# Shift and scale sums of the mixer stages by transposes inside the fourth and the eighth merge block

## The reference

```
mods_x = split(silu(c)     @ ada_w[l] + ada_b[l], 9)     # shift, scale, gate of the three sublayers
mods_c = split(silu(c_ctx) @ ada_w[l] + ada_b[l], 9)
h = layer_norm(s) * (1 + scale) + shift
s = layer_norm(ALPHA * s + w * gate * f(h)) * ln_w + ln_b
```

```
y = (sigmoid(g_ret) * y_ret + sigmoid(g_na) * y_na + sigmoid(g_fou) * y_fou) @ w_o
```

## Time and profile before

| | |
|---|---|
| median of three runs | 2575.18 us |
| the profiled execution | 2576.9 us, span 2575.0 us |
| PE busy | 2453.0 us, 95% of the span |
| DVE busy | 1609.2 us, 62% |
| ACT busy | 936.9 us, 36% |
| shares of the chain that ended last | PE 87%, DVE 8%, ACT 3% |
| mean granted clock of TensorE | 0.975 |

### The profile page before, as it was taken

How to read it: one execution, slowest core, us unless ns; L and a number is a source line. 1 busy time by engine, 2 the same in 40 slices (tenths; PEclk the granted TensorE clock), 3 DMA queues, 4 the chain that set the end, 5 groups by cost and what they waited for, 6 DMA issues and landing times.

```text
span 2575.0 us, 33634 instructions
## 1 busy us (share of the span) xinstructions
PE 2453.0 (95%) x13530; PEld 2120.2 (82%) x13530; DVE 1609.2 (62%) x2146; ACT 936.9 (36%) x1361; POOL 126.0 (5%) x163
## 2 busy tenths in 40 slices
PE   6999999997999999979999999999999899996998
PEld 6988988986876788869889888889888786995996
DVE  4566668756465544576666686666686554665655
ACT  2522355432114322244223554224554223443443
POOL 2000001000001000010000010000020001001000
PEclk9999999999999999989999999999999998997999
DMA  8455555651122343345455565455555242674763
GB/s 263 144 169 166 193 190 175 174 170 33 49 90 58 109 136 123 127 151 164 150 177 194 187 200 173 155 180 188 180 181 173 66 139 70 194 250 131 226 202 123
DMA packets 476814, 400.62 MB, mean 156 GB/s; under 512 B 36340, under 2 KB 428788, under 8 KB 476404
## 3 DMA queue, kind: packets, MB, share of 16 engines
q1 hardware_dynamic: 464992, 391.18, 47.9%
q10 hardware_dynamic: 11668, 7.30, 0.9%
HBM read 397.25 MB, written 1.17 MB: 155 GB/s over the span
## 4 chain that ended last, share of the span: by engine, by line
PE 87%; DVE 8%; ACT 3%; issue 2%; DMA 1%; ACTq 0%; SPq 0%; POOL 0%; POOLq 0%; DVEq 0%
PE ps L1327 25%; PE ps L1328 25%; PE ps L1329 25%; DVE wl L835 2%; PE ps L1585 2%; PE ps L1576 1%; PE ps L1597 1%; PE ps L1525 1%; ACT tB L524 1%; PE ps L1352 1%; ACT wh L506 1%; PE ps L1678 1%; DVE st L893 1%; PE ps L1359 1%; PE ps L1367 1%
## 5 line engine op out<-in xcount | busy, mean ns | idle before, releaser
L835 DVE TENSOR_TENSOR wl<-raw,wh 128x1024 fp32r<-128x1024 f32 x576 | 701.3, 1221 | 678.1 <-ACT wh L506 676.8
L506 ACT ACTIVATE wh<-raw 128x1024 fp32r<-128x1024 f32 x576 | 609.8, 1059 | 1290.1 <-PE ps L1329 1256.9
L1327 PE MATMUL ps<-hh,wh 128*128 128x256 f32 (+1 forms) x2736 | 897.0, 328 | 32.6 <-DVE hl L926 19.8
L1328 PE MATMUL ps<-hl,wh 128*128 128x256 f32 (+1 forms) x2736 | 889.0, 325 | 0.0
L1329 PE MATMUL ps<-hh,wl 128*128 128x256 f32 (+1 forms) x2736 | 888.8, 325 | 0.0
L1327 PEld LDWEIGHTS ps<-hh,wh 128*128 128x128 f32 x2736 | 525.2, 192 | 78.5 <-DVE hl L926 20.9
L1328 PEld LDWEIGHTS ps<-hl,wh 128*128 128x128 f32 x2736 | 525.2, 192 | 41.7 <-issue 1.0
L1329 PEld LDWEIGHTS ps<-hh,wl 128*128 128x128 f32 x2736 | 524.9, 192 | 41.2
L850 DVE SCALAR_TENSOR_TENSOR acc<-araw,c,acc 128x1024 f32<-128x1024 f32 x210 | 258.4, 1280 | 36.3 <-DMA araw<-in_ada_w 34.8
L1327 PE MATMUL ps<-wh,stage_h_f 128*128 128x512 f32 x616 | 240.8, 391 | 2.0 <-DVE stage_l_f L979 2.0
L1328 PE MATMUL ps<-wl,stage_h_f 128*128 128x512 f32 x616 | 239.7, 389 | 0.0
(11 more groups left out here) (160 smaller groups left out, 2388.8 us busy)
## 6 DMA issues: line engine op xcount, KB each, us to landing
raw<-in_ffa_w SPq DMA_DIRECT2D x204, 512.0 KB, 3.6
raw<-in_ffb_w SPq DMA_DIRECT2D x168, 512.0 KB, 3.9
raw<-in_mix_w_in SPq DMA_DIRECT2D x148, 512.0 KB, 4.0
araw<-in_ada_w SPq DMA_DIRECT2D x136, 512.0 KB, 5.1
raw<-in_mix_w_o SPq DMA_DIRECT2D x24, 512.0 KB, 4.3
raw<-in_ret_w_out SPq DMA_DIRECT2D x16, 512.0 KB, 4.0
raw<-in_na_fou_w_out SPq DMA_DIRECT2D x16, 512.0 KB, 3.9
raw<-in_ada_w SPq DMA_DIRECT2D x8, 512.0 KB, 5.2
```

The lines of the kernel that those rows point to most:

```text
L506: A.activation(wh[:, s, :], raw[:, s, :], ACT.Copy).then_inc(w_rounded, 1)
L835: V.tensor_tensor(wl[:, s, :], raw[:, s, :], f(wh[:, s, :]), ALU.subtract).then_inc(w_split, 1)
L1327: T.matmul(out, a[0], b[0], start=start, stop=False)
L1328: T.matmul(out, a[0], b[1], start=False, stop=False)
```

## The change

In both mixers the sums of shift and scale go over to transposes and a DVE sum, one stream at a time, and both are moved into a merge block:

- PE, in blocks `mm` = 3 (shift) and `mm` = 7 (scale): behind unit v, it waits until all of the sum's steps are in `acc` and turns stream 0's eight pieces into banks 6 and 7. Behind unit v+2 it does the same for stream 1, once DVE has taken stream 0 out of the banks (semaphore `mod_taken`). In layer 1 there is stream 0 only.
- DVE, in the same blocks: behind the first gated product it sums stream 0 along the free axis (`mixer_mods`), behind two more splits stream 1, and adds the bias.
- The 16 or 8 one-column matmuls in the fourth block and those behind the eighth go, with their waits. `down` waits for both sums at its start, since its first tile uses banks 6 and 7.

```diff
+            def mixer_mods(i, w, st):
+                t = i + 1
+                ns = htiles(t) // LT
+                c = t % 3 * 3 * KD + w * KD
+                dve.wait_ge(ada_mm, ada_sums(i) + gate_halves(i + 1) - gate_halves(i) + w * ns + st + 1)
+                y = ps[:, 6:8].rearrange("p a n -> p (a n)").rearrange("p (k n) -> p k n", k=KD)
+                V.tensor_reduce(modT[:, t % 2, w, :, st], y, AXX, ALU.add).then_inc(mod_taken, 1)
+                if st == ns - 1:
+                    dve.wait_ge(mod_taken, 4 * (i // 3) + (w + 1) * ns)
+                    ...
+                    V.tensor_tensor(m, m, b, ALU.add).then_inc(mods_ready, 1)
...
                     gated(0, z, 1, 2)
+                    if mm in (3, 7):
+                        mixer_mods(i, mm // 4, 0)
                     split(v + 6)
                     split(v + 7)
+                    if mm in (3, 7) and htiles(i + 1) == NT:
+                        mixer_mods(i, mm // 4, 1)
...
-                    if mm == 3:
-                        next_mods(i, 0, 6)
-                    if mm == 7:
-                        next_mods(i, 1, 2)
-                    else:
+                    if mm < 7:
                         for n in range(2):
                             ada(i, MERGE_ADA + 2 * mm + n)
...
+            def mixer_turn(i, w, st):
+                pe.wait_ge(ada_step, ada_ops[ada0(i) + (w + 2) * KD])
+                before = 4 * (i // 3) + w * (htiles(i + 1) // LT) + st
+                if before:
+                    pe.wait_ge(mod_taken, before)
+                for k in range(KD):
+                    ins = T.transpose(ps[:, 6 + k // 4, (k % 4) * P:(k % 4 + 1) * P], acc[:, st, k * P:(k + 1) * P], ident[:])
+                ins.then_inc(ada_mm, 1)
...
                 if i % 3 == 1:
                     pe.wait_ge(g_sum, 5 + 40 * l + 5 * (KD - 1) + 1)
-                    pe.wait_ge(mods_ready, 2 * (i + 1) + 1)
+                    pe.wait_ge(mods_ready, 2 * (i + 2))
...
                     form_a(v, 0, src, N)
+                    if mm in (3, 7):
+                        mixer_turn(i, mm // 4, 0)
                     pe.wait_ge(g_sum, smn + 1)
...
                     form_a(v + 2, 2, src, N)
-                    if mm == 3:
-                        ada_mods(i, 0, 6)
+                    if mm in (3, 7) and htiles(i + 1) == NT:
+                        mixer_turn(i, mm // 4, 1)
...
-                pe.wait_ge(g_sig, 24 * l + 3 * (KD - 1) + 5)
-                ada_mods(i, 1, 2)
                 down(i, AT["wo", l], KD)
```

More of the change, by code:

```diff
@@ L227, in trunk @@
         ada_step, adab_turned, adab_copied, adab_ready = [sem(n) for n in ("ada_step", "adab_turned", "adab_copied", "adab_ready")]
-        gbias_in, first_mm, ada_mm, gate_ready, mods_ready = [sem(n) for n in ("gbias_in", "first_mm", "ada_mm", "gate_ready", "mods_ready")]
+        gbias_in, first_mm, ada_mm, mod_taken, gate_ready, mods_ready = [sem(n) for n in ("gbias_in", "first_mm", "ada_mm", "mod_taken", "gate_ready", "mods_ready")]
         y_tile, ln_in, post_stat, post_rstd, x_ready = [sem(n) for n in ("y_tile", "ln_in", "post_stat", "post_rstd", "x_ready")]
@@ L345, in chunk_streams, with mod_sums @@
             return streams(s) if w == 2 else htiles(s) // LT
+        def mod_sums(i):
+            return htiles(i + 1) // LT if i % 3 == 1 else 1
         def ada_sums(i):
-            return 1 + gate_halves(i) + 2 * i
+            return 1 + gate_halves(i) + sum(mod_sums(j) for j in range(i)) * 2
         MERGE_ADA = KD + 2
@@ L845, in ada @@
                         if m:
-                            dve.wait_ge(ada_mm, ada_sums(i) + (0, gate_halves(i + 1) - gate_halves(i), gate_halves(i + 1) - gate_halves(i) + 1)[n // KD])
+                            dve.wait_ge(ada_mm, ada_sums(i) + (0, gate_halves(i + 1) - gate_halves(i), gate_halves(i + 1) - gate_halves(i) + mod_sums(i))[n // KD])
                         ins = V.tensor_scalar(acc[:, st], araw[:, m % AR], c, None, ALU.mult)
@@ L884, in turned_mods @@
                 V.tensor_tensor(m, m, b, ALU.add).then_inc(mods_ready, 1)
-            def next_mods(i, w, bank):
-                dve.wait_ge(ada_mm, ada_sums(i + 1) - 1 + w)
-                take_mods(i + 1, w, bank, float(DV))
+            def mixer_mods(i, w, st):
[7 more added lines that the diff above has]
+                    dve.wait_ge(mod_taken, 4 * (i // 3) + (w + 1) * ns)
+                    m = modT[:, t % 2, w, :, 0:ns]
+                    b = adaT[:, t // 3, c:c + KD].unsqueeze(2).broadcast_to([P, KD, ns])
+                    V.tensor_tensor(m, m, b, ALU.add).then_inc(mods_ready, 1)
             def stats(src, which, t, done):
@@ L1412, in down @@
                             pe.wait_ge(g_sum, 5 + 40 * (l + 1))
-                            pe.wait_ge(mods_ready, 2 * (i + 2))
                         else:
```

## The result

The changed kernel takes 2598.23 us (median of 4 runs, 2597.30 to 2598.62) against 2574.85 us (2570.20 to 2578.59) of the kernel before on the same chip: a ratio of 1.0091, with a 95% interval of 1.0074 to 1.0109. It is slower, as forecast (2593.0 us), by 23.4 us in place of 17.8, and 0.23 us above the upper end of the range (2598).

The account below looks back on a forecast made before the run. PE, busy 95% of the span, was taken to bound the kernel. Terms of +1.6, +6.4, +4.0 and +5.8 us at four places summed to +17.8 us, giving a median of 2593.0 us, range 2584 to 2598 us.

Parts of the forecast that it names:

- The wait: Behind unit v in four merge blocks, PE waits for DVE's last sum steps: 3.40 to 3.58 us each, 13.97 us together.
- Transposes against one-column matmuls: In the merge blocks, eight transposes add 0.87 us; removed one-column groups give back 5.20 and 1.78 us in the fourth blocks.
- Start of `down`: Behind the eighth blocks, removed matmuls become a wait for `stage_l_m`; 0.37 us won in layer 0, nothing in layer 1.
- The clock: Behind each of the four new PE waits, a new clock drop costing 1.5 us, bounds nothing and 1.72 us.
- A second term: The two existing clock drops at the start of `down` were let stand, with no change in time.
- Rival 1: At the four places the waits come but the new clock drops don't: +11.8 us, 2587.0 us; chance 0.15.
- Rival 2: Transposes count as quiet time, adding two more 1.5 us low-clock stretches in layer 0: +20.8 us, 2596.0 us; chance 0.09.
- Rival 3: DVE's sums come onto the path, two to four of 1.215 us showing: about 2596.5 us; chance 0.06.
- Rival 4: Sums are in time behind unit v, so no waits: -2.1 us, 2573.1 us, or 2569.7 us; chance 0.05.

Follow-up runs that it names:

- second profile of the changed kernel: The changed kernel run once more with nothing altered, against the kernel before: 2596.99 us, ratio 1.0086.
- the one with the first sum one split earlier: Transposes moved behind units v+2 and v+3, with DVE's stream 0 sum between the splits of v+6 and v+7, against the kernel before: 2576.28 us, ratio 1.0000.
- the first moved version: Changed kernel with transposes moved behind units v+2 and v+3, DVE's stream 0 sum behind the split of v+7: 2590.79 us, ratio 1.0059 to the kernel before.

## Why the prediction was right, and where it was wrong

- **The wait** (forecast 13.97 us): right. It came at the four places, from the releaser named: 13.0 us in PE's idle records, 13.6 us by the starts of the products. With the wait alone added to the old kernel the places lose 20.0 us; with the wait removed by place they win 2.9.
- **Transposes against one-column matmuls**: right. 0.79 us for eight at full clock (forecast 0.87), and one-column matmuls of 1.70 us in the fourth block of layer 1 (forecast 1.78: the first product behind them takes 0.20 us, not 0.12); the two errors cancel, and the two fourth blocks without a wait measured -3.52 and -0.93 us where the terms give -3.46 and -0.91.
- **Start of `down`**: right. 2.96 us of waiting in both layers (forecast 3.1), and almost nothing was won by taking the matmuls away: from the first product of the last unit to the first of `down` it is 8.56 us in place of 8.93 in layer 0, the 0.37 us of the forecast, and 6.00 in place of 6.01 in layer 1.
- **The clock**: this is the step that failed, in size. "I take 1.5 us for each of the four waits" gave 6.0 us. The three short drops measured 1.7 us each, and the fourth 2.9: 8.0 us. In the second profile of the changed kernel the four drops make 6.5 us (three of 1.7, one of 1.4).

  The 1.5 was read too low. It lay between rows that showed 1.45 to 1.72, and the nearest in kind, a clean wait, was put at 1.58. But its window of the earlier trace rows stopped before the clock had risen. Read whole, that drop is like the others, 3.41 us at 0.50, a loss of 1.7 us:

```profile
588.01:591.42 3.41, 3.41 (x10) 0.50 0.00 0
```

  With 1.7 us for each wait the sum is +18.6 us, what the second profile shows. The first has 1.2 us more for the long drop.

  A second term stood at nothing: that the drops which are there already would stay as they were. The +0.9 us left over in layer 0 is such a one. Near the end of `down` every kernel has a wait of PE of 2.8 us and, 5.5 us later, one of 3.2 to 3.9 us. In the kernel before, the clock falls behind the second alone; in the changed one it falls behind the first and stays low past the second:

```profile
1130.72:1134.13 3.41, 3.36 (x8) 0.50 0.53 154
```

```profile
1132.19:1142.43 10.24, 7.04 (x18) 0.50 0.36 103
```

  The long form is in both profiles of the changed kernel, in the one with three times the transposes and in the one with the first sum one split earlier, the short form in the other six. What decides between them was not tested.
- **The range**: its upper end took in no change of clock in stretches that the change does not touch. These moved the profiled execution by +1.9 us, and the clock lost there varies by up to 14 us between profiled executions. This is why the time came out above the range: the stretches give +19.9 us, inside it, and the other 3.5 us of the 23.4 between the medians do not. A forecast of the places that is right to 1 or 2 us still meets a spread of this size; with the sum at 2593.0 the end should have stood a few us higher. Ten runs of the changed kernel span 2589.5 to 2602.8.
- **Rival 1** (no new drops, 2587.0) fell: all eight waits of the two profiles had one behind them. **Rival 2** (transposes as quiet time) is mostly not borne out: the wait alone gives the same drops, and filler in place of the wait removes them though the transposes stay. The Trainium skill, "TensorE: Matmul & The Clock Gate", Part 4, has transposes not counting as busy PE time in the same way. Here 8 to 16 of them in a dense stretch left the clock at 1.00; behind a wait, one drop in four was long with 24 of them, and one in four or none with 8. **Rival 3** (DVE's sums on the path) was not seen in the changed kernel, but it is what befell the first moved version, through a wrong place on DVE. **Rival 4** fell with the waits.
- **Open**: the places account for 18.6 to 19.9 us, the ratios for 22.1 to 23.4. Both profiles of the changed kernel lost 5 to 7 us more clock in the rest of the program than the one of the kernel before, but so did the version without the four waits. Clock is not all of it either: of the 3.7 us between the layers 2.2 are PE standing still. Whether the other 3 us are chance or an effect of the change on when the later waits and drops fall, I did not settle.

## What to carry to other kernels

When work is moved ahead on a full engine, look up when its inputs are really ready: the moved group paid 3.3 us of waiting and 1.7 us of clock at each of four places, for a saving of 0.9 and 3.5 us at two of them, and two units later the same group waited for nothing. And when the price of a drop is read from a window, the window must reach from where the clock falls to where it rises. Work that stands in a stretch where its engine waits anyway (the scale's sum before `down`) costs next to nothing and should stay there; moving it frees only idle time. When a consumer is moved, check what stands ahead of it in its own queue, not only what it waits for itself.

## What the runs showed of the hardware

- A wait of PE of 3.2 to 3.3 us in a dense stretch was followed by half clock in 16 of 16 cases (four profiles of three kernels), and one of 3.7 us in 2 of 2 (transposes moved down). One of 2.9 to 3.4 us at the start of `down` was followed by it in 9 of 12, and the one of 2.8 us near the end of `down` in layer 0 in 4 of 10.
- A short drop loses about 1.7 us of work, 3.4 us at half rate (1.2 GHz), whichever product follows. Some are twice as long, 6.8 us; which ones, changed between executions of one kernel. In the first profile of the changed kernel the long one had already begun inside the wait, where PE did nothing:

```profile
2323.00:2324.54 1.54, 0.00 (x0) 0.64 0.61 239
```

- One-column matmuls over 3.5 us did not hold the clock up: it fell behind them in the kernel before, while through 1.8 us of them it stayed at 1.00. 15 matmuls of 512 columns over the same time held it at 1.00.
